# Other byte offsets for column-form weights in their SBUF slots

## What is computed

```python
proj = rms_norm(x, norm_g) @ w_in             # 2048 x 16512
mk, mv = split(rms_norm(mem, mem_norm_g) @ w_mem_kv)
merged = (sigmoid(ga) * (ya @ w_up_a) + sigmoid(gb) * (yb @ w_up_b)
          + sigmoid(gc) * (yc @ w_up_c))
x = x + merged @ w_o
proj = rms_norm(x, norm1_w) @ w_in_2          # 2048 x 15376
mixed = g0 * (o_a @ w_br_attn) + g1 * (o_g @ w_br_gla) + g2 * (y_c @ w_br_conv)
x = x + mixed @ w_out
h2 = rms_norm(x, norm2_w)
x = x + (silu(h2 @ w_ffn_gate) * (h2 @ w_ffn_up)) @ w_ffn_down
return rms_norm(x, final_norm_w)
```

## Time and profile before

| | before |
|---|---|
| median of three runs | 2927.6 us |
| profiled execution | 2924.8 us |
| its span, first to last instruction | 2923.1 us |
| TensorE busy | 2886.3 us (99%) |
| DVE busy | 1607.1 us (55%) |
| ACT busy | 1340.5 us (46%) |
| mean granted TensorE clock | 0.998 |
| read from HBM | 513.39 MB |

### The profile page before, as it was taken

How to read it: one execution, slowest core, us unless ns; L and a number is a source line. 1 busy time by engine, 2 the same in 40 slices (tenths; PEclk the granted TensorE clock), 3 DMA queues, 4 the chain that set the end, 5 groups by cost and what they waited for, 6 DMA issues and landing times.

```text
span 2923.1 us, 42673 instructions
## 1 busy us (share of the span) xinstructions
PE 2886.3 (99%) x18226; PEld 2493.8 (85%) x18226; DVE 1607.1 (55%) x1850; ACT 1340.5 (46%) x1527; POOL 73.3 (3%) x173
## 2 busy tenths in 40 slices
PE   7999999999999999999999999999999999999998
PEld 7979888888988888898998899888888888888886
DVE  5564665656656556554555466554654544544444
ACT  5442543544554454444445454444444444444443
POOL 5000000001000000000000000000000000000000
PEclk9999999999999999999999999999999999999999
DMA  7443444566665656656556665666656666666664
GB/s 210 129 144 113 131 131 120 163 191 186 223 196 184 188 157 194 195 160 191 169 162 198 174 168 162 201 197 194 195 181 195 190 191 188 190 191 202 194 194 151
DMA packets 356178, 518.30 MB, mean 177 GB/s; under 512 B 18288, under 2 KB 137220, under 8 KB 355220
## 3 DMA queue, kind: packets, MB, share of 16 engines
q1 hardware_dynamic: 355220, 512.37, 59.0%
q0 software_dynamic: 768, 3.20, 0.4%
HBM read 513.39 MB, written 2.11 MB: 176 GB/s over the span
## 4 chain that ended last, share of the span: by engine, by line
PE 98%; DVE 1%; ACT 1%; DMA 0%; issue 0%; SPq 0%; DVEq 0%; ACTq 0%
PE gp L1618 23%; PE gp L1620 23%; PE gp L1619 23%; PE gp L1627 7%; PE gp L1629 7%; PE gp L1628 7%; PE ps L1794 4%; PE ps L1676 1%; PE ps L1751 1%; PE ps L1782 1%; DMA gain<-in_norm_g 0%; PE ps L1772 0%; PE ps L1736 0%; DVE w_lo L1029 0%; PE ps L1987 0%; PE ps L2004 0%
## 5 line engine op out<-in xcount | busy, mean ns | idle before, releaser
L1029 DVE TENSOR_TENSOR w_lo<-w_raw,w_hi 128x1024 fp32r<-128x1024 f32 (+2 forms) x976 | 1166.9, 1202 | 971.4 <-ACT w_hi L641 967.0
L641 ACT ACTIVATE w_hi<-w_raw 128x1024 fp32r<-128x1024 f32 (+2 forms) x976 | 1011.1, 1041 | 1119.0 <-PE gp L1620 887.8
L1618 PE MATMUL gp<-w_hi,h_hi 128*128 128x512 f32 x2112 | 833.0, 394 | 1.5 <-DVE w_lo L1029 1.5
L1620 PE MATMUL gp<-w_lo,h_hi 128*128 128x512 f32 x2112 | 822.8, 390 | 0.0
L1619 PE MATMUL gp<-w_hi,h_lo 128*128 128x512 f32 x2112 | 822.2, 389 | 0.0
L1627 PE MATMUL gp<-h_hi,w_hi 128*128 128x256 f32 x1696 | 487.4, 287 | 2.4 <-DVE h_lo L1094 2.4
L1629 PE MATMUL gp<-h_hi,w_lo 128*128 128x256 f32 x1696 | 472.9, 279 | 0.0
L1628 PE MATMUL gp<-h_lo,w_hi 128*128 128x256 f32 x1696 | 472.9, 279 | 0.0
L1618 PEld LDWEIGHTS gp<-w_hi,h_hi 128*128 128x128 f32 x2112 | 396.6, 188 | 83.7 <-DVE w_lo L1029 1.9
L1620 PEld LDWEIGHTS gp<-w_lo,h_hi 128*128 128x128 f32 x2112 | 396.5, 188 | 83.6
L1619 PEld LDWEIGHTS gp<-w_hi,h_lo 128*128 128x128 f32 x2112 | 396.7, 188 | 80.7 <-issue 0.5
(11 more groups left out here) (283 smaller groups left out, 1785.5 us busy)
## 6 DMA issues: line engine op xcount, KB each, us to landing
w_raw<-in_w_in SPq DMA_DIRECT2D x384, 512.0 KB, 4.1
w_raw<-in_w_ffn_gate SPq DMA_DIRECT2D x88, 512.0 KB, 4.4
w_raw<-in_w_ffn_up SPq DMA_DIRECT2D x88, 512.0 KB, 4.4
w_raw<-in_w_ffn_down SPq DMA_DIRECT2D x88, 512.0 KB, 4.1
w_raw<-in_w_in SPq DMA_DIRECT2D x136, 256.0 KB, 3.2
w_raw<-in_w_in SPq DMA_DIRECT2D x128, 192.0 KB, 3.1
w_raw<-in_w_mem_kv SPq DMA_DIRECT2D x32, 512.0 KB, 4.3
w_raw<-in_w_o SPq DMA_DIRECT2D x32, 512.0 KB, 4.3
```

The costliest lines, as they stand in the source:

```text
L641: act.activation(in_slot(w_hi, n), w_raw[:, slot, 0:size], ACT.Copy).then_inc(sem("hi_done"), 1)
L1029: dve.tensor_tensor(in_slot(w_lo, n), w_raw[:, slot, 0:size], in_slot(w_hi, n).bitcast(F32), ALU.subtract)\
L1618: pe.matmul(o, xh, wh, start=(k == 0), stop=False)
L1620: ins = pe.matmul(o, xh, wl, start=False, stop=(k == last_k))
```

## The change

Only the table of shifts is another. In bytes, wide blocks go from 192 to 96, pair from 192 to 32, trio from 192 to 160, narrow from 192 to 64; row-form blocks stay at 0. The sizes of all buffers, their addresses, the order of all instructions and the values computed are the same.

```diff
-SHIFT = {'rows': 0, 'wide': 48, 'pair': 48, 'trio': 48, 'narrow': 48}
+SHIFT = {'rows': 0, 'wide': 24, 'pair': 8, 'trio': 40, 'narrow': 16}
```

## The result

| | before | after |
|---|---|---|
| median | 2927.38 us (11 runs, 2924.97 to 2929.20) | 2935.75 us (11 runs, 2933.64 to 2936.54) |
| ratio to before | | 1.0031, 95% interval 1.0023 to 1.0038 |
| profiled execution, span | 2924.8, 2923.1 us | 2935.8, 2934.1 us |

The account below looks back on a forecast made before the run. TensorE was taken to bound the kernel. Column-form gains of 8.3, 1.1, 3.4, 3.1 and 3.0 us made 18.9; counting 6 of the 8.3 left 16.6, so 2927.6 - 16.6 = 2911.0 us, range 2907 to 2939.

Parts of the forecast that it names:

- What bounds the kernel: TensorE, busy 99% of a 2923.1 us span; the moved address is used only by column-form matmuls and what fills their operands.
- Two paces, kept from stop to stop: Column-form matmuls start 113.3 ns (quick) or 117.8 ns (slow) apart, and a stretch keeps its pace until the next stop.
- 85% slow: Share of column-form matmuls before the change read as running at the slow pace, from mean durations; some 15% quick.
- ACT, DVE and DMA at nothing: ACT's copy, DVE's subtraction and the DMAs into w_raw were taken to neither gain nor lose from the new shifts.
- I take the quick pace for most of the work: Column-form matmuls at the new shifts mostly start 113.3 ns apart, saving 4.45 ns each, 16.6 us counted; chance 0.47.
- the terms of 8.3, 1.1, 3.4, 3.1 and 3.0 us: Gains before 560 us, in cross-attention, Q, L and down, and convolution; together 18.9 us, with 6 of the 8.3 counted.
- Rival 1: The address plays no part in column form; the time stays within some 3 us of 2927.6; chance 0.30.
- Rival 2: Weight loads meet streaming h worse: 4.45 ns more on all 5088 matmuls, quick 15% lost, 2953.6 us; chance 0.23, mixed included.
- threshold of 1.2 ns: Extra time per column-form matmul from which the slower case decides, 5.9 us over 5088 matmuls.
- in only one of the kinds, 2932 to 2940: Slower case hitting just one block kind, 2932 to 2940 us; a third of the slower case's 0.23.
- The chances: Quick pace mostly 0.47 (2911 us), no effect 0.30 (2927.6 us), slower 0.23, a third of it mixed below 2940.
- The range: Whole-kernel time from 2907 to 2939 us, leaving out the full slower case and a few per cent at the bottom.

## Why the prediction was wrong, step by step

- **What bounds the kernel** held. TensorE's column form is all that the address reaches; row form has 226.7 ns as before, ACT and DVE have their durations, and the chain is the same.
- **Two paces, kept from stop to stop** held for the kernel before and served well as a reading; other distances have other paces. "85% slow" agrees with a count of the starts (15% of the steps quick), and by stage, in the prediction's order, the count gives 98, 75, 94, 82 and 64% slow where 95, 67, 100, 85 and 58 were read. But the way to it, from mean durations, worked by luck: the kernel at 64 bytes reads longer durations and has shorter steps.
- **ACT, DVE and DMA at nothing** held, and the two kernels with moved activations show that the address matters within TensorE's own reads.
- **"I take the quick pace for most of the work"** is the step that failed, and with it the terms of 8.3, 1.1, 3.4, 3.1 and 3.0 us. It rested on 96, 32 and 160 bytes being alike, 32 off a multiple of 64. They are not: 118.4, 118.3 and 119.9 ns. None has a quick pace at all, and what quick steps the kernel before had, 15%, were lost. In the convolution blocks, where 36% of the steps had been quick and the place chosen is one of the two worst of thirteen, the loss was 4.0 us where a gain of 3.0 had been booked.
- **Rival 1, the address has no part** is out by 120.0 against 113.3 ns. The Trainium skill's two independent read ports ("TensorE: Matmul & The Clock Gate", Step-by-step) may be so, but the time of a matmul does depend on how the two reads lie to each other; the runs decide. The lines of 16 bytes of the Trainium skill ("SBUF — State Buffer", Specifications) do not account for it either: 0, 64 and 160 bytes are all multiples of 16, and 56 and 72, which are not, are no worse than their neighbours 48 and 80.
- **Rival 2, slower** was what happened, through its own mechanism, at another price: 1.56 ns a step on average instead of one more step of 4.45 on all and the loss of the quick ones. Its threshold of 1.2 ns was right, and the mixed form "in only one of the kinds, 2932 to 2940" holds the time, though all three large kinds lost: by stage 0.8 us in the recurrent part, 0.6 in C, 1.0 in L, 4.0 in the convolution.
- **The chances** gave 0.47 to a sign for which the only evidence was arithmetic on offsets. The trace showed one distance for column form. It could say that there was room on both sides, and not on which side three new values would fall.
- **The range** held the time because the slower case had been let in up to 2939.

## What to carry to other kernels

Where a stream of weight loads and matmuls bounds a kernel, the distance in bytes between the two operands is a parameter worth a sweep in steps of 8 to 16 bytes: here it moves a 256-column matmul between 113.3 and 120.0 ns, and the whole kernel between 0.998 and 1.005. Sweep one form at a time, since row and column form want different distances, and do not reason from one value to its neighbours. Read the pace from the starts of a long stretch, and compare only stretches of full granted clock.

## What was not expected

- A 64-byte move of the activations costs 40 us, 1.4%, in row form alone (233.5 ns against 226.7). The alignment of h at 256 bytes is worth more than the whole span of column-form offsets, 21 us.
- At one distance a stretch may run at one of two steady paces (113.3 or 117.8 at 64 bytes and at 192) or of three (117.3, 118.7 or 120.0 at 96), fixed at the stop before it. At 64 bytes 53 of 124 stretches are quick, at 192 12 of 126, each in its one traced execution. The nine executions at 64 bytes spread over 7.1 us, from 2916.9 to 2924.1, and the traced one took 2922.5; whether the share differs from one execution to the next was not looked at. What the stop decides was not found; a first step of 0.30 us or of 0.20 us leads to either.
- Most of the Q stage is one stretch of 670 steps, at 117.8 ns both at 64 bytes and before. At the quick pace it would save, as an estimate, 670 x 4.45 = 3.0 us; a way to start it anew was not tried.
- The granted clock at the start and ahead of the Q blocks came back at other times in some profiled executions (0.94 or 0.83 over 30 us), worth up to 1.9 us at each place. It did so at good and bad distances alike: 0.94 at 64 bytes and in the kernel before, but also with the convolution kind alone at 160.
